# Cross attention of a two-block transformer kernel: queries, keys, values and turned weights in high and low halves

## What is computed

```python
def memory_cross_attention(h, m, w_q, w_kv, w_o):
    q = (h @ w_q).reshape(Bn, S, X_HEADS, X_HEAD_DIM)       # 4 heads of 256, S = 256
    k, v = jnp.split(m @ w_kv, 2, axis=-1)                  # 256 rows of memory
    s = jnp.einsum('bshd,bmhd->bhsm', q, k).astype(jnp.float32) * (X_HEAD_DIM ** -0.5)
    p = jax.nn.softmax(s, axis=-1).astype(v.dtype)
    o = jnp.einsum('bhsm,bmhd->bshd', p, v).reshape(Bn, S, D_MODEL)
    return o @ w_o

# in the block:
    x = x + rms_norm(y, post_mix_g[l])                      # y: gated unit, MoBA attention, conv, @ w_out
    h = rms_norm(x, pre_x_g[l]); m = rms_norm(mem, mem_g[l])
    x = x + rms_norm(memory_cross_attention(h, m, w_xq[l], w_xkv[l], w_xo[l]), post_x_g[l])
```

## Time and profile before

| What | Value |
|---|---|
| median of 3 runs | 766.45 us (766.09 to 768.27) |
| the profiled execution | 765.89 us |
| its span, first to last instruction | 764.1 us |
| mean granted clock of TensorE | 0.998 |
| TensorE busy | 754.7 us (99%) |
| weight loads on TensorE | 657.2 us (86%) |
| VectorE busy | 515.5 us (67%) |
| ScalarE busy | 400.7 us (52%) |
| GpSimd busy | 70.1 us (9%) |
| chain that ended last, share on TensorE | 90% |

### The profile page before, as it was taken

How to read it: one execution, slowest core, us unless ns; L and a number is a source line. 1 busy time by engine, 2 the same in 40 slices (tenths; PEclk the granted TensorE clock), 3 DMA queues, 4 the chain that set the end, 5 groups by cost and what they waited for, 6 DMA issues and landing times.

```text
span 764.1 us, 10439 instructions
## 1 busy us (share of the span) xinstructions
PE 754.7 (99%) x4313; PEld 657.2 (86%) x4313; DVE 515.5 (67%) x583; ACT 400.7 (52%) x506; POOL 70.1 (9%) x79
## 2 busy tenths in 40 slices
PE   9999999999999999999999999999999999999997
PEld 8988888888988888888899888789887988888885
DVE  5758965685756666565769999774647655656554
ACT  6467387543644554544653586673546534444442
POOL 3000003030000000000233322030002000000000
PEclk9999999999999999999999999999999999999999
DMA  9754555345566555665566535365245565555431
GB/s 308 229 176 156 176 209 200 133 156 175 172 236 197 166 166 171 202 208 203 169 211 198 163 130 201 113 237 181 69 122 181 166 220 198 188 179 191 160 131 56
DMA packets 74287, 135.66 MB, mean 178 GB/s; under 512 B 4458, under 2 KB 28928, under 8 KB 74240
## 3 DMA queue, kind: packets, MB, share of 16 engines
q1 hardware_dynamic: 72304, 130.80, 51.0%
q10 hardware_dynamic: 1936, 4.19, 1.6%
HBM read 133.93 MB, written 1.05 MB: 177 GB/s over the span
## 4 chain that ended last, share of the span: by engine, by line
PE 90%; DVE 6%; ACT 1%; issue 1%; POOL 1%; DVEq 0%; POOLq 0%
PE wide L1966 63%; PE bank L1966 24%; DVE arena L1402 3%; PE bank L2084 3%; DVE low L1296 1%; ACT arena L704 1%; POOL low L557 1%; ACT high L704 0%; DVE arena L1530 0%; DVE arena L1667 0%; DVE neg_max L1672 0%; DVE x L1736 0%; POOL var L564 0%; DVE xn L1757 0%; DVE tiny L1638 0%
## 5 line engine op out<-in xcount | busy, mean ns | idle before, releaser
L1296 DVE TENSOR_TENSOR low<-raw,high 128x2048 fp32r<-128x2048 f32 (+1 forms) x116 | 262.0, 2278 | 119.1 <-ACT high L704 117.9
L704 ACT ACTIVATE high<-raw 128x2048 fp32r<-128x2048 f32 (+1 forms) x130 | 234.5, 1821 | 127.0 <-PE wide L1966 99.1
L1966 PE MATMUL wide<-act_hl,high 128*128 128x256 f32 (+1 forms) x1184 | 297.2, 330 | 0.0
L1966 PE MATMUL wide<-act_hl,low 128*128 128x256 f32 x832 | 235.9, 283 | 0.1
L1966 PEld LDWEIGHTS wide<-act_hl,high 128*128 128x128 f32 x1184 | 200.2, 191 | 22.3
L1966 PE MATMUL wide<-high,act_hl 128*128 128x512 f32 (+1 forms) x560 | 176.1, 389 | 0.8 <-DVE act_hl L1375 0.6
L1966 PEld LDWEIGHTS wide<-act_hl,low 128*128 128x128 f32 x832 | 158.4, 190 | 1.1 <-issue 0.2
L1966 PEld LDWEIGHTS wide<-high,act_hl 128*128 128x128 f32 x560 | 104.2, 188 | 24.0 <-issue 3.1
L1966 PE MATMUL wide<-low,act_hl 128*128 128x512 f32 (+1 forms) x280 | 107.6, 384 | 0.0
L1966 PE MATMUL bank<-high,hid_l 128*128 128x512 f32 x216 | 84.8, 393 | 0.2 <-DVE hid_l L1595 0.2
L1966 PE MATMUL bank<-high,hid_h 128*128 128x512 f32 x216 | 84.4, 391 | 0.0
(11 more groups left out here) (205 smaller groups left out, 653.8 us busy)
## 6 DMA issues: line engine op xcount, KB each, us to landing
raw<-in_w_ff_dram SPq DMA_DIRECT2D x32, 1024.0 KB, 5.2
raw<-in_w_in_dram SPq DMA_DIRECT2D x28, 1024.0 KB, 5.4
raw<-in_w_ffn_in_dram SPq DMA_DIRECT2D x44, 512.0 KB, 4.9
raw<-in_w_ffn_out_dram SPq DMA_DIRECT2D x11, 1024.0 KB, 6.9
raw<-in_w_xkv_dram SPq DMA_DIRECT2D x8, 1024.0 KB, 5.1
raw<-in_w_o_dram SPq DMA_DIRECT2D x4, 1024.0 KB, 4.9
raw<-in_w_out_dram SPq DMA_DIRECT2D x4, 1024.0 KB, 5.1
raw<-in_w_xq_dram SPq DMA_DIRECT2D x4, 1024.0 KB, 5.1
```

The lines of the kernel that those rows point to most:

```text
L704: return act.activation(dst, src, func, **k)
L1296: tt(part(low, g), part(raw, g), f32(part(high, g)), SUB).then_inc(sem.low_by_dve, 1)
L1966: return pe.matmul(dst, lhs, rhs, start=start, stop=stop, skip_group_check=loose)
```

## The change

Keys, values, queries and the turned weights are kept as a high half in float32r and a low half, and the scores and values are made with `mm3`, three passes, instead of one float32 product each.

- `kv_in` on ScalarE writes the high half. A new `kv_low` on VectorE subtracts it from the bank, two steps of 128x512 for each chunk. TensorE waits for `kv_low` where it waited for `kv_in`.
- The queries go out of the banks unscaled but for 1/16: ScalarE copies the high half (`xq_high`), VectorE makes the low (`xq_low`). The queries' inverse root is instead the scale of the exponential; `x_max` gets a second small step that multiplies the maximum by it. `norm_diag(4)`, `rep_made`, `rep_out` and `rep_wait` for the queries are gone.
- `x_turned` has a second part on VectorE that subtracts, and TensorE's `x_out` waits for that (`x_tl`) instead of ScalarE's copy (`x_t`).
- The low keys and the queries lie in `hid1_h`, `hid1_l`, `hid_h` and `hid_l`, the others in the arena.

The diff, without the lines that only declare the three new semaphores:

```diff
@@ -301,12 +304,14 @@
         soft = sb("soft", [P, 16])
 
 
+        arena_at = nc.sbuf_base
         arena = sb("arena", [P, ARENA])
+        arena_r = nc.alloc_sbuf_tensor_at("arena_r", [P, ARENA], F32R, offset=arena_at)
         top = [0]
 
-        def carve(*shape):
+        def carve(*shape, home=arena):
             size = math.prod(shape)
-            a = arena[:, top[0]:top[0] + size]
+            a = home[:, top[0]:top[0] + size]
             top[0] += size
             assert top[0] <= ARENA, top[0]
             if len(shape) == 2:
@@ -315,6 +320,22 @@
                 a = a.rearrange("p (a b c) -> p a b c", a=shape[0], b=shape[1])
             return a
 
+
+        def rounded(*shape):
+
+            return carve(*shape, home=arena_r)
+
+        def k_low(kt):
+
+            return (hid1_h + hid1_l)[kt // 2][:, kt % 2, :]
+
+        def q_high(kt):
+
+            return hid_h[kt // 4][:, kt % 4, :]
+
+        def q_low(kt):
+
+            return hid_l[kt // 4][:, kt % 4, :]
 
         y = carve(6, T)
         gates = carve(TT, 3 * D)
@@ -364,8 +385,9 @@
         top[0] = 0
         spatial_w = carve(4, P)
         spatial_t = carve(4, P)
-        k_mem = carve(KD, T)
-        v_mem = carve(TT, D)
+        k_high = rounded(KD, T)
+        v_high = [rounded(TT, NB)]
+        v_low = [rounded(TT, NB)]
         attn = top[0]
         sc = carve(8, DIAG)
         pt = carve(4, DIAG)
@@ -385,8 +407,10 @@
         post_junk = carve(TT, D)
         top[0] = attn
         x_p = carve(4, TT, T)
-        x_pt = carve(4, TT, T)
-        x_q = carve(KD, T)
+        x_pt_high = rounded(4, TT, T)
+        x_pt_low = rounded(4, TT, T)
+        v_high.append(rounded(TT, NB))
+        v_low.append(rounded(TT, NB))
 
         wide = ctx.enter_context(nc.psum_tensor("wide", [P, 4, NB], F32))
         bank = [wide[:, i, :] for i in range(4)]
@@ -1007,10 +1031,12 @@
 
             def kv_in(c):
                 if c < 2:
-                    copy_pair(k_mem[:, 4 * c:4 * c + 2, :], k_mem[:, 4 * c + 2:4 * c + 4, :], sem.kv_in)
+                    copy_pair(k_high[:, 4 * c:4 * c + 2, :], k_high[:, 4 * c + 2:4 * c + 4, :], sem.kv_in)
                 else:
-                    a = (c - 2) * NB
-                    copy_pair(v_mem[:, 0, a:a + NB], v_mem[:, 1, a:a + NB], sem.kv_in)
+                    copy_pair(v_high[c - 2][:, 0, :], v_high[c - 2][:, 1, :], sem.kv_in)
+
+            def xq_high(c):
+                copy_pair(hid_h[c][:, 0:2, :], hid_h[c][:, 2:4, :], sem.xq_high, 1 / 16)
 
             def qk2_in(i):
                 d = (q2, k2)[i]
@@ -1091,14 +1117,14 @@
                     act.wait_ge(sem.x_max, me.seen("x_max"))
                     for t in range(TT):
                         k = 2 * h + t
-                        ins = f(x_p[:, h, t, :], bank[4 + h][:, t * T:(t + 1) * T], ACT.Exp, bias=neg_max[:, k:k + 1],
-                                accum_out=soft[:, k:k + 1])
+                        ins = f(x_p[:, h, t, :], bank[4 + h][:, t * T:(t + 1) * T], ACT.Exp, scale=rstd[:, 8 + t:9 + t],
+                                bias=neg_max[:, k:k + 1], accum_out=soft[:, k:k + 1])
                     ins.then_inc(sem.x_p, 1)
 
             def x_turned(i):
                 for h in (2 * i, 2 * i + 1):
                     act.wait_ge(sem.x_turned, me.seen("x_turned"))
-                    f(flat(x_pt[:, h, :, :]), bank[4 + h][:, :], ACT.Copy).then_inc(sem.x_t, 1)
+                    f(flat(x_pt_high[:, h, :, :]), bank[4 + h][:, :], ACT.Copy).then_inc(sem.x_t, 1)
 
             def x_out(i):
                 act.wait_ge(sem.w_used, me.used)
@@ -1242,10 +1268,11 @@
             norm_stat(4)
             kv_in(3)
             ahead_of(("xq", 0), "C")
-            rep_out()
+            xq_high(0)
             ahead_of_half(("xq", 1), 0)
             x_exp(0)
             ahead_of_half(("xq", 1), 1)
+            xq_high(1)
             x_turned(0)
             x_exp(1)
             x_out(0)
@@ -1767,11 +1794,39 @@
                         stt(x[:, t, cut], xn[:, t, cut], rstd[:, k:k + 1], x[:, t, cut], MUL, ADD)\
                             .then_inc(sem.x_ready, 1)
 
+            def kv_low(c, pair):
+
+                for i, b in enumerate(pair):
+                    dve.wait_ge(sem.kv_in, me.seen("kv_in"))
+                    if c < 2:
+                        kt = 4 * c + 2 * i
+                        h_ = k_high[:, kt:kt + 2, :]
+                        l_ = (hid1_h + hid1_l)[kt // 2][:, :, :]
+                        tt(l_, in2(b[:, :]), f32(h_), SUB).then_inc(sem.kv_low, 1)
+                    else:
+                        tt(v_low[c - 2][:, i, :], b[:, :], f32(v_high[c - 2][:, i, :]), SUB).then_inc(sem.kv_low, 1)
+
+            def xq_low(c):
+                for i, b in enumerate(me.pair()):
+                    dve.wait_ge(sem.xq_high, me.seen("xq_high"))
+                    k = slice(2 * i, 2 * i + 2)
+                    stt(hid_l[c][:, k, :], in2(b[:, :]), 1 / 16, f32(hid_h[c][:, k, :]), MUL, SUB).then_inc(sem.xq_in, 1)
+
+            def x_turned(i):
+                for h in (2 * i, 2 * i + 1):
+                    dve.wait_ge(sem.x_t, me.seen("x_t"))
+                    tt(flat(x_pt_low[:, h, :, :]), bank[4 + h][:, :], f32(flat(x_pt_high[:, h, :, :])), SUB)\
+                        .then_inc(sem.x_tl, 1)
+
             def x_max(i):
+                if i == 0:
+                    dve.wait_ge(sem.rstd, me.seen("rstd", TT))
                 for h in (2 * i, 2 * i + 1):
+                    m = neg_max[:, 2 * h:2 * h + 2]
                     dve.wait_ge(sem.x_s, me.seen("x_s"))
-                    dve.tensor_reduce(neg_max[:, 2 * h:2 * h + 2], in2(bank[4 + h][:, :]), AX.X, MAX, negate=True)\
-                        .then_inc(sem.x_max, 1)
+                    dve.tensor_reduce(m, in2(bank[4 + h][:, :]), AX.X, MAX, negate=True).then_inc(sem.dve_step, 1)
+                    dve.wait_ge(sem.dve_step, me.step())
+                    tt(m, m, rstd[:, 8:8 + TT], MUL).then_inc(sem.x_max, 1)
 
             def x_norm(i):
                 for h in (2 * i, 2 * i + 1):
@@ -1883,6 +1938,7 @@
             ahead_of_half(("kv", 0), 0)
             norm_split(2)
             ahead_of_half(("kv", 0), 1)
+            kv_low(0, me.pair())
             ahead_of("zc", "C")
             zc_in()
             ahead_of("q2", "C")
@@ -1907,11 +1963,13 @@
             low_of_bank(1, b=bank[4])
             spatial()
             group_mean()
+            kv_low(1, me.pair(1))
             low_of_bank(0, b=bank[7])
             group_norm()
             ahead_of(("mix_top", 0), "T")
             group_silu()
             group_norm_low()
+            kv_low(2, me.pair(1))
             ahead_of(("mix_top", 1), "T")
             low_of_bank(2, b=bank[5])
             ahead_of(("mix_bottom", 0), "T")
@@ -1920,19 +1978,20 @@
             post_last(0)
             ahead_of(("kv", 3), "T")
             norm_split(4)
-            norm_diag(4)
+            kv_low(3, me.pair())
             ahead_of(("xq", 0), "C")
-            rep_wait()
-            scaled_in((x_q[:, 0:2, :], x_q[:, 2:4, :]), sem.xq_in, 1 / 16)
+            xq_low(0)
             ahead_of_half(("xq", 1), 0)
             x_max(0)
             x_norm(0)
             ahead_of_half(("xq", 1), 1)
-            scaled_in((x_q[:, 4:6, :], x_q[:, 6:8, :]), sem.xq_in, 1 / 16)
+            xq_low(1)
+            x_turned(0)
             x_max(1)
             x_norm(1)
             x_out(0)
             ahead_of_half(("xo", 0), 0)
+            x_turned(1)
             x_out(1)
             ahead_of_half(("xo", 0), 1)
             post_first()
@@ -2381,8 +2440,9 @@
                     pe.wait_ge(sem.xq_in, h + 1)
                     for t in range(TT):
                         for k in range(2):
-                            ins = mm(bank[4 + h][:, t * T:(t + 1) * T], x_q[:, 2 * h + k, t * P:(t + 1) * P],
-                                     k_mem[:, 2 * h + k, :], start=k == 0, stop=k == 1)
+                            kt, tok = 2 * h + k, slice(t * P, (t + 1) * P)
+                            ins = mm3(bank[4 + h][:, t * T:(t + 1) * T], q_high(kt)[:, tok], q_low(kt)[:, tok],
+                                      k_high[:, kt, :], k_low(kt), k == 0, k == 1)
                     ins.then_inc(sem.x_s, 1)
 
             def x_turn(i):
@@ -2395,13 +2455,14 @@
                     ins.then_inc(sem.x_turned, 1)
 
             def x_out(i):
-                pe.wait_ge(sem.x_t, me.seen("x_t", 2))
+                pe.wait_ge(sem.x_tl, me.seen("x_tl", 2))
                 for h in (2 * i, 2 * i + 1):
                     for c in range(2):
                         for m in range(2):
-                            ch = slice((2 * h + c) * P, (2 * h + c + 1) * P)
-                            ins = mm(bank[4 + h][:, c * T:(c + 1) * T], v_mem[:, m, ch], x_pt[:, h, m, :],
-                                     start=m == 0, stop=m == 1)
+                            a = (2 * h + c) % 4 * P
```

(13 more changed lines are left out.)

3 lines of the change are left out of this document (added).

## The result

| | before | after |
|---|---|---|
| median of the runs that were made together | 768.02 us (5 runs, 766.09 to 768.27) | 778.87 us (5 runs, 777.61 to 781.22) |
| the profiled execution | 765.89 us | 779.06 us |
| its span | 764.1 us | 777.3 us |
| mean granted clock | 0.998 | 0.993 |

After / before is 1.0149, with a 95% interval of 1.0128 to 1.017. The changed kernel is slower by about 11.4 us (9.8 to 13.1); the two medians alone differ by 10.9, because the executions of a kernel lie at two levels of time, some 1.5 us apart; an early fall of the clock, met further down, goes with them. The prediction was 777.5 us, 11.6 over the profiled execution that it started from. The two spans differ by 13.2 us, and that is what I take apart here.

A forecast was written before the change was run, and what follows sets the result against it. The prediction took TensorE's nearly hole-free matmul stream to bound the kernel: 765.9 - 1.6 (cross attention) + 10.1 (two TensorE stops on VectorE's subtractions) + 3.1 (clock) = 777.5 us, range 772.5 to 781.

The forecast's parts named there:

- The bottleneck and the two stops: TensorE bounds; waiting for `kv_low`, it stands 3.0 us before `mix_top` 0 and 7.1 before `mix_top` 1, together 10.1.
- Rival 3: Group norm's chain does not shift with the first stop: stops total 7.0 us, time 773.1 or less; chance 0.1.
- The clock behind the second stop: After the 7.1 us stop before `mix_top` 1 the clock falls, costing 1.8 us (1.2 to 2.4).
- The clock behind the first stop: After the 3.0 us stop before `mix_top` 0 the clock may fall; 1.3 us taken (0 to 2.4).
- the clock's sum: Loss from falls of the granted clock behind both TensorE stops: 3.1 us, between 0 and 4.8.
- rival 1: After the stops the clock stays or costs almost nothing: 774.4 us; chance 0.2.
- The cross attention: Shorter products and no `rep_made`: 0.45 + 0.57 + 0 + 0.55 = 1.6 us less, between 1.1 and 3.0.
- Scores of heads 0 and 1: In the cross attention, 8 float32 products of 3.45 us become 24 passes of 2.88 us: 0.57 us less.
- The middle: Heads 2 and 3's scores with heads 0 and 1's values: 1.36 us saving taken as 0; later starts offset it.
- The last stretch: Values of heads 2 and 3: 0.55 of 0.58 us gained; first-channel subtraction ends just when the matmuls do.
- Three passes for one product: Three split passes of 0.12 us, weight load included, take 0.36 us against 0.43 for one float32 product.
- The calls taken at zero: Calls 0 and 3 of the keys' and values' subtractions: VectorE holes or a late TensorE request make their cost 0.

The follow-up runs named there:

- the waits alone: The kernel before, with only TensorE waits ahead of `mix_top` 0 and 1 for second `group_mean` step and `group_norm_low`, without subtractions; 777.64 us against 767.61, ratio 1.0139.
- the first pair moved: Changed kernel with only the second keys' subtractions moved ahead, between the weight splits before `low_of_bank(1)`; 774.93 us, ratio 1.01 to the kernel before.
- the values' pair moved: Changed kernel with only the first values' subtractions moved to directly before `group_norm`; 769.73 us, ratio 1.003 to the kernel before; profiled twice more: 769.93 and 769.91 us.
- the filled second stop: Changed kernel with 22 small identity products (44 records) on TensorE before `mix_top` 1, while it waits for the values' subtraction; 777.03 us, ratio 1.0122 to the kernel before.
- the interleaved order: Both subtraction pairs moved, plus head 0's cross-attention output taken out ahead of head 3's exponential and normalising; 765.18 us, ratio 0.9979 to the kernel before.
- both pairs moved: Changed kernel with keys' subtractions between the weight splits before `low_of_bank(1)` and values' directly before `group_norm`; 765.3 us against the kernel before's 766.61, ratio 0.9978.

## Why the prediction was right, step by step

**The bottleneck and the two stops: right.** They were worked out as 10.1 us and took 9.96. The first: TensorE was to stand from 475.82 to 478.84; it starts its matmuls at 480.90 in a run of the program that is 2.13 us late by then, so 2.95 later than before, for 3.0. The second was to be 7.1; it is 9.96 - 2.95 = 7.0. The argument that the group norm's chain shifts with the first stop held as well: the reciprocal starts 5.18 us later than in the earlier trace rows, of which 2.13 are the late start and 3.05 the shift. Moving one pair at a time (3.06 and 6.99 us) and the kernel with the waits alone (7.7 of the 9.96) show that it is the place in VectorE's list; before them this was only read from the order.

**Rival 3: half right.** It said that with the first stop gone 7.0 us would remain, and that is what the kernel with the first pair moved has. As a case of this change it fell, since the root did wait for `group_var`.

**The clock behind the second stop: 1.8 predicted, 2.16 measured.** Within the 1.2 to 2.4 given. In two other kernels stops of 5.8 and 6.9 us cost 2.8 and 3.0. Those are over the upper end, which came from how long TensorE may have run low at the start of the span; that was too short a stretch to bound it. The length of the stop does not set the loss: 6.9 us cost 2.16 once and 3.02 once. In all three the loss is about half of the time from TensorE's first matmul to the return of the clock: 2.16 us of 4.1 (after), 2.80 of 5.5 (the waits alone) and 3.02 of 5.9 (the keys' pair moved), read from the mean clock of short windows.

**The clock behind the first stop: 1.3 predicted, 0 measured.** This is the step that failed. It rested on the fall 2.1 us after the last matmul; a stop of 3 us seemed longer than that. In none of five profiles with this stop (after, with the values' pair moved three times, with the filled second stop) did the clock fall there, and in all three with an unfilled stop of 5.8 to 6.9 us it did. That it can't fall in such a stop is not shown: in those three it fell 4.2 (after), 4.4 (the waits alone) and 2.6 us (the keys' pair moved) after the last matmul, and a stop of 2.8 us is longer than the last of these. The Trainium skill (page "TensorE: Matmul & The Clock Gate", section "HAM oscillation — how this bites in real kernels") says that a TensorE that is made to wait between groups of matmuls falls to the lower clock; the traces here agree for the second stop. The first stop is shorter than the waits of the section's example, a TensorE that waits for long transfers; the prediction laid the rule on both stops alike, which the section does not, and so had no reason from it to price the first. The row of the span's end, from which the fall was read, shows a TensorE with no more work to come and not a stop with matmuls behind it. The bounds of the clock's sum, 0 to 4.8, do not fit their parts either: 1.2 to 2.4 and 0 to 2.4 add up to 1.2 to 4.8, and the 0 belongs to rival 1.

**The cross attention: 1.6 predicted, 1.0 measured.** Term by term: `rep_made` -0.45 predicted, -0.44 measured: 22.73 us for 11.21 + 0.45 + 11.51, the first of which is this row of before.

```profile
509.44 11.21 PE wide L1966 x72
```

Scores of heads 0 and 1 -0.57, measured -0.62 (2.83 for 3.45). The middle 0, measured +0.27: TensorE is on the scores of heads 2 and 3 0.54 us later after the projection (555.61 and its subtraction, then 556.36), and from there to `xo` it takes 0.27 less. Two exponentials of head 3, each 0.09 longer than before, lie on this path. The mechanism is the one predicted, a copy and a subtraction ahead of the scores and a wait on L1567 behind them, and the interleaved order shows that 0.77 us could be had there. The last stretch -0.55, measured -0.28, and this is the term that was mis-sized. I had the subtraction of the first output channels end just when the shorter matmuls do. But only the half of the products that makes head 2's output is ahead of that subtraction, and only that half brings it forward:

```profile
571.96 0.69 DVE L1567 SCALAR_TENSOR_TENSOR act_hl<-bank,act_hl 128x512 fp32r<-128x512 f32 x1 [3.39 <-ACT act_hl L728]
```

It ends at 572.65, and the next matmul of `xo` starts at 572.71. What TensorE saves in the other half, head 3's products, it spends waiting for this step, so 0.28 of 0.55 remains.

**Three passes for one product: right.** The Trainium skill's load of some 107 ns for each pass (page "TensorE: Matmul & The Clock Gate", section "LDWEIGHTS (loading the stationary operand)"), which the prediction set against it, does not lie bare: 24 passes take 2.83 us, 0.12 each with the load, and going back to float32 makes the kernel about 1.5 us slower by the chain.

**The calls taken at zero: right.** No wait on `kv_low` of calls 0 and 3 shows among TensorE's waits, and from the end of `mix_top` 1 to `xq` 0 the kernel takes 19.80 us for 19.86.

**The base.** The sum was made against an execution without the early fall. The one that was profiled after has it, 1.6 us, and some 0.5 us of a late weight at the start. Without these 2.13 us the spans differ by 11.06, for 11.6 predicted; the ratio says 11.4. The closeness is in part luck: the clock was put 0.9 too high (3.1 for 2.16) and the gain of the cross attention 0.6 too high (1.6 for 1.0), and these two errors work against each other, with 0.1 too much for the stops. What the prediction earned is the stops, 10.1 for 9.96, which are most of the sum.

**A version that beats both.** With both pairs moved, 765.3 us for 766.61, 0.22% under the kernel before (0.13 to 0.31) and about 13 us under the changed one. With the cross attention interleaved as well, the chain is 0.77 us shorter still.

## What to carry to other kernels

When the release of a buffer moves from one engine to another, look at what stands ahead of the releasing step in the new engine's list before looking at how long the step is: here four steps of about 0.65 us cost 10 us and the clock 2 more, 7.7 of the 10 for the place alone, and moving two calls gave all of it back. A stop on the bounding engine shifts every chain that starts from it, so two late releases must be worked out one after the other and not added up from the trace of before. A gain in shorter matmuls counts only up to the next step of another engine that they wait for, so split such a gain at each of those steps before adding it.

## What the runs showed of the hardware that was not expected

- The granted clock can fall while TensorE works without a hole. Near 67 us, 0.4 to 1.4 us behind 8 matmul records that fill 4 rows (1.97 us), it goes to 0.50 for 3.4 us with TensorE busy for 3.00 of 3.00, and costs 1.6 us. It is in 7 of 12 profiles, among them those of kernels that don't differ ahead of it, and in the kernels with ten runs or more the profiled execution lies at the upper level when it has the fall and at the lower one when it does not (for the kernel before the levels are 766.1 to 766.6 and 767.3 to 768.2 in the 27 executions beside the kernel with both pairs moved). The cause is open.
- A stop of 2.8 to 3 us did not bring the clock down in 5 profiles, one of 5.8 to 6.9 did in all 3, and the loss behind it was 2.2 to 3.0 us. The fall came 2.6, 4.2 and 4.4 us after the last matmul. Matmuls with the identity in the stop prevented it (1 profile).
- ScalarE's exponential with a scale of its own for each row takes 0.56 us over 128x256, and 0.47 us with a constant one. It was predicted at 0 to 0.1 and costs 0.09 each; it stands on the path in the chain for head 3 alone, two of them.
